# Attention kernel: the first three weight chunks of the pool projection are split in units 8, 11 and 14 instead of 5, 7 and 12

## The reference

```
s = einsum('bhqd,bhkd->bhqk', qb, kp) * scale          # 8 heads of width 64, 128 queries at a time
s = s + c[:, :, q0:q1, None] - cp[:, :, None, :]       # c: running sum of log sigmoid(forget logits)
s = where(mask, s, -1e30)
p = softmax(s, axis=-1)
outs.append(einsum('bhqk,bhkd->bhqd', p, vp))
...
y_pool = pool_mixer(u_pool, pool_w, pool_scale) @ w_pool_out     # (1024, 512) @ (512, 1024)
x = x + (g_pool * y_pool + g_fox * y_fox) @ w_out
```

## Time and profile before

| | |
|---|---|
| median of 3 runs | 1445.1 us (1444.64 to 1445.21) |
| profiled execution, its own time | 1444.98 us |
| its span, first to last instruction | 1443.1 us |
| PE busy | 98% of the span |
| DVE, ACT, POOL busy | 67%, 43%, 39% |
| mean granted TensorE clock | 0.997 of full speed (0.997 x 2.4 GHz) |
| units 0 to 31 | about 336 to 505 us of the span |

### The profile page before, as it was taken

How to read it: one execution, slowest core, us unless ns; L and a number is a source line. 1 busy time by engine, 2 the same in 40 slices (tenths; PEclk the granted TensorE clock), 3 DMA queues, 4 the chain that set the end, 5 groups by cost and what they waited for, 6 DMA issues and landing times.

```text
span 1443.1 us, 19379 instructions
## 1 busy us (share of the span) xinstructions
PE 1419.4 (98%) x7065; PEld 1171.6 (81%) x7065; DVE 971.6 (67%) x1393; ACT 618.4 (43%) x1169; POOL 557.9 (39%) x572
## 2 busy tenths in 40 slices
PE   8999999999999999999999999999999999999998
PEld 5878888887688888888888788888888888888886
DVE  7745495646877754327666887777677676775767
ACT  6545343526876642116543533332233322444445
POOL 5743233334555301005011755444444443354402
PEclk9999999999999999999999999999999999999999
DMA  8265263555333145114113213333233334883333
GB/s 213 58 120 124 54 141 86 74 103 194 111 112 114 47 161 204 59 45 146 30 44 117 74 59 110 110 109 109 83 108 109 110 110 180 310 290 96 94 103 146
DMA packets 105911, 168.45 MB, mean 117 GB/s; under 512 B 7469, under 2 KB 63297, under 8 KB 104410
## 3 DMA queue, kind: packets, MB, share of 16 engines
q1 hardware_dynamic: 99032, 147.13, 34.7%
q0 software_dynamic: 3200, 11.57, 2.2%
q10 hardware_dynamic: 3586, 8.52, 1.6%
HBM read 123.32 MB, written 42.30 MB: 115 GB/s over the span
## 4 chain that ended last, share of the span: by engine, by line
PE 89%; POOL 3%; ACT 3%; DVE 3%; issue 1%; DMA 1%; SPq 0%; DVEq 0%; ACTq 0%; POOLq 0%
PE ps L2198 27%; PE ps L2200 27%; PE ps L2199 27%; PE ps L2401 2%; PE ps L2410 1%; PE ps L2439 1%; ACT prob L1265 1%; PE ps L2440 1%; DMA raw_f<-in_w_in 1%; PE ps L2205 1%; PE ps L2269 1%; DVE prob L1801 1%; POOL w_lo L831 0%; PE ps L2574 0%; POOL tok_f L877 0%
## 5 line engine op out<-in xcount | busy, mean ns | idle before, releaser
L2198 PE MATMUL ps<-t_lo,s_hi 128*128 128x512 f32 x308 | 119.9, 389 | 0.1
L2199 PE MATMUL ps<-t_hi,s_hi 128*128 128x512 f32 x308 | 119.8, 389 | 0.0
L2200 PE MATMUL ps<-t_hi,s_lo 128*128 128x512 f32 x308 | 119.8, 389 | 0.0
L2198 PE MATMUL ps<-h_lo_T,w_hi 128*128 128x512 f32 x256 | 100.5, 393 | 1.3 <-ACT u_t L1176 1.0
L1524 DVE TENSOR_TENSOR s_lo<-w_raw,s_hi 128x512 fp32r<-128x512 f32 x77 | 59.1, 768 | 60.3 <-ACT s_hi L1439 60.1
L2200 PE MATMUL ps<-h_hi_T,w_lo 128*128 128x512 f32 x256 | 99.7, 389 | 0.0
L2199 PE MATMUL ps<-h_hi_T,w_hi 128*128 128x512 f32 x256 | 99.6, 389 | 0.0
L1439 ACT ACTIVATE s_hi<-w_raw 128x512 fp32r<-128x512 f32 x77 | 48.7, 632 | 117.7 <-PE ps L2200 99.1
L1455 ACT ACTIVATE p_sb<-ps 128x512 f32<-128x512 f32 x22 | 13.1, 598 | 189.3 <-PE ps L2200 189.3
L2198 PE MATMUL ps<-hf_lo_T,w_hi 128*128 128x512 f32 x212 | 82.5, 389 | 0.0
L2199 PE MATMUL ps<-hf_hi_T,w_hi 128*128 128x512 f32 x212 | 82.5, 389 | 0.0
(11 more groups left out here) (381 smaller groups left out, 4307.0 us busy)
## 6 DMA issues: line engine op xcount, KB each, us to landing
w_raw<-hs_dram SPq DMA_DIRECT2D x77, 256.0 KB, 2.8
raw_p<-in_w_ffn_in SPq DMA_DIRECT2D x22, 512.0 KB, 4.6
w_raw<-in_w_ffn_in SPq DMA_DIRECT2D x22, 512.0 KB, 4.3
hs_dram<-h_sum SPq DMA_DIRECT2D x11, 1024.0 KB, 8.9
hs_dram<-hq SPq DMA_DIRECT2D x11, 768.0 KB, 7.0
wq_B<-in_w_ffn_out SPq DMA_DIRECT2D x8, 1024.0 KB, 7.2
raw_f<-in_w_in SPq DMA_DIRECT2D x14, 512.0 KB, 7.2
gate_dram<-c_st SPq DMA_DIRECT2D x28, 256.0 KB, 2.2
```

The lines of the kernel that those rows point to most:

```text
L2198: nc.tensor.matmul(dst, w_h, x_l, start=start, stop=False, skip_group_check=onto)
L2199: nc.tensor.matmul(dst, w_h, x_h, start=False, stop=False, skip_group_check=onto)
L2200: return nc.tensor.matmul(dst, w_l, x_h, start=False, stop=stop, skip_group_check=onto)
```

## The change

It edits two tables and nothing else. Chunks 0, 1 and 2 of the pool projection's weights get their high part on ACT at the end of units 8, 11 and 14, where it was 5, 7 and 12. Their low part on POOL follows at the end of the same unit; it was 5, 8 and 12. SP's raw loads of chunks 2, 3 and 4 go by the same table and move to the same units. Chunks 3 to 6 keep their units 18, 23 (low part 24), 28 and 32.

```diff
-SPLIT_AT = {5: 0, 7: 1, 12: 2, 18: 3, 23: 4, 28: 5, 32: 6}
-LOW_AFTER = {5: 0, 8: 1, 12: 2, 18: 3, 24: 4, 28: 5}
+SPLIT_AT = {8: 0, 11: 1, 14: 2, 18: 3, 23: 4, 28: 5, 32: 6}
+LOW_AFTER = {8: 0, 11: 1, 14: 2, 18: 3, 24: 4, 28: 5}
```

## The result

| | before | after |
|---|---|---|
| median of 6 runs each | 1445.16 us (1444.64 to 1445.58) | 1451.82 us (1448.03 to 1452.95) |
| ratio, 95% interval | | 1.0041 [1.0029, 1.0053] |
| profiled execution | 1444.98 us | 1450.61 us |
| its span | 1443.1 us | 1448.8 us |
| PE, DVE busy | 1419.4 and 971.6 us | 1422.6 and 977.3 us |

The change makes the kernel 6.7 us slower. The forecast was 1446.4 us with 1448.2 as the end of its range. In a later group of runs the changed kernel had 1449.7 us (1447.99 to 1451.58, 7 runs) against 1445.7, so 4.0 us more, ratio 1.003 [1.0019, 1.004]. It is slower each time; and its executions lie 4.9 and 3.6 us apart in the two groups, those of before 0.9 and 4.0 (2.0 without its one slowest).

A forecast was written before the change was run, and what follows sets the result against it. PE, busy 98% of the span, was taken as the bound, so only its waits count. Terms -1.41 + 0.6 + 0.85 + 0.7 + 0.6 = +1.3 us gave 1446.4 us on the median; range 1443.5 to 1448.2 us.

The forecast's parts named there:

- The credit of unit 8: Units 5 to 8: removing chunk 0 and chunk 1's high part ends PE waits; 1.41 us gained, bounds 1.72 and 0.7.
- the copies' wait at 365.81: PE's 0.35 us wait for ACT's copies for unit 6, claimed to go without the high part at 360.97.
- Chunks 0 and 1: New places in units 8 and 11: low parts on POOL hold DVE, costing PE 0.6 and 0.85 us.
- PE's waits near 390 and 398: Sign in the profile after: these PE waits should be 0.6 and 0.9 us longer than before.
- Chunk 2's hold on k: Unit 14: the low part on POOL holds DVE's k pair, delaying unit 16's scores; cost 0.7 us, bounds -0.16 and 1.2.
- What stands behind chunk 2 on POOL: Unit 16: negc row load leaves near 415.0, so bias, za and PE's fill are late; cost 0.6 us, bounds 0 and 2.5.
- Slower, by the load behind chunk 2: Rival, unit 15: negc load waits for DVE's scalings and shares with chunk 4's load; fill waits 3.1 us, 1448.9 us; chance 0.11.
- The credit stays: Rival: new places at units 9, 12 and 15 cost PE nothing, -1.4 to -1.7 us remain, 1443.6 us; chance 0.27.
- nothing reaches PE: Rival: what the moved work delays is covered in old and new places alike, time stays at 1445.1 us; chance 0.08.
- the chance of over 0.2%: Whole kernel: chance 0.11 of being slower by more than 0.2% (2.9 us), against 0.86 for within 0.2%.

The follow-up runs named there:

- chunk 4 late, again: Kernel after the change, with SP's raw load of chunk 4 issued in unit 16 instead of 14, second group of runs: 1450.31 us, ratio 1.0032.
- behind: Kernel before, with POOL issuing unit 16's negc row load only once both DVE scalings of unit 15 are done: 1451.37 us, ratio 1.0035.
- chunk 2 alone: Kernel before, with only chunk 2 moved to unit 14, chunks 0 and 1 left in their old places: 1451.72 us, ratio 1.0043.
- the version with units 8, 12 and 15: Kernel after, with chunk 1 moved to unit 12 and chunk 2 to unit 15, chunk 0 still in 8: 1444.35 and 1444.59 us, ratios 0.9994 and 0.9995.

## Why the prediction was wrong

**The credit of unit 8: right.** -1.41 predicted, -1.28 in the profile. My 363.75 for the end of unit 6's k pair fits (363.52 + 1.40 - 1.18 = 363.74): the waits for k and for the scaled probabilities are gone there, and ACT is late next with 0.54 us where I had 0.31. Of the copies' wait at 365.81, which I had go, 0.47 us stand at 366.81; without it PE would have come sooner to the values at 373.26, where it waits for ACT anyway.

**Chunks 0 and 1: right in kind, too dear.** DVE was held where the prediction put it: the scaling of unit 9 took 1.21 us instead of 0.51 and the q instruction of unit 12 took 1.45 instead of 0.68. What reached PE is 0.24 us where I had 0.6 and 0.66 where I had 0.85. The slack that I counted half took more. I had PE's waits near 390 and 398 grow by 0.6 and 0.9 us; the first stayed at 1.42, the second grew by 0.66.

**Chunk 2's hold on k: right.** 0.69 us against 0.7; the pair took 2.86 us instead of 1.40. The Trainium skill, SBUF — State Buffer, section "Who interferes with whom", has it that a DVE instruction with two inputs in SBUF contends with a GpSimd instruction that reads SBUF, over a port pair that is locked and not shared out, and that one with at most one input there, outside the two-port modes, does not. The q and the k rows agree, and so does the bias, which reads the scores in PSUM and kept its length in the earlier trace rows. The scaling, held as well, reads one tile; that it is held rests on its row alone (1.21 us at 381.93 against 0.51).

**What stands behind chunk 2 on POOL: this step failed, in two parts.** The load went out at 416.19 - 1.18 = 415.01, just as predicted (415.0). But I let it land after the 4.28 us of before, and put the sharing of the DMA engines into the bounds only. It took 5.55 us, 1.27 more. Another 0.43 of the difference is that PE came to the fill earlier than I had it (0.31 us late where I had 0.74), since the terms of chunks 0 and 1 were smaller, and 0.27 is the way from bias to `za` and fill. 0.6 + 1.27 + 0.43 + 0.27 = 2.57, as in the profile. It lay just outside the bound of 2.5 that I had named. I named chunk 4's load as what could share, and missed the second one: q's load, released by the k pair that the same low part holds, so that both are in the air with the row by construction. By the landings q's load weighs at least as much (5.5 to 6.0 us with q alone, 5.12 with chunk 4 alone).

The second part stands nowhere in the prediction: **a wait of about 2 us or more on PE can cost the clock.** In the profile that is 1.54 us, and 1.3 to 2.5 us up to unit 18 in the seven profiles that had it. I had priced the rival's wait of 3.1 us at 3.1 us. With the terms of the profile the sum is -1.28 + 0.24 + 0.66 + 0.69 + 2.57 = +2.88 without the clock, which is 1448.0 us and still inside the range, and +4.42 with it, 1449.5, which is outside. The median of the first group, 6.7 us above, needs more than this one profile shows, and no profile of such an execution was taken. A longer landing and a clock that stays low for 6.8 us would give it: "chunk 4 late, again", "behind" and "chunk 2 alone" had such a clock and took 5.8, 5.6 and 6.9 us more than before between unit 5 and unit 18.

**The rivals.** "Slower, by the load behind chunk 2" had the place, the engine and nearly the wait (2.33 to 3.81 us against 3.1), and its chance of 0.11 was far too low. Its first reason, that the issue waits for the scalings, is refuted for the landing: 5.59 and 5.57 us beside scalings on DVE and on ACT. The rule of the Trainium skill that I gave for it (SBUF — State Buffer, section "SBUF: two separate sides") shows here as no more than 0.6 us of issuing, 1.70 against 1.10 us, and not in the landing. Its second reason, chunk 4's load beside it, is part of the answer. "The credit stays" and "nothing reaches PE" fell at 391, 399 and 416 us. What I got wrong in the chances is that the steps up to unit 15 could only add up to small sums, while the one behind chunk 2 had its far bound 4 times its value and nothing of the trace against it; there the value should have lain nearer to 2 than to 0.6, and the chance of over 0.2% near a half.

**Left open.** Landings come from one profile per kernel and differ by up to 1.5 us within a group, so the shares of q and chunk 4 are known in order only. That the clock falls in one execution and not in the next of the same kernel is seen, not explained. The 1.0 us of the version with units 8, 12 and 15 stands in both its profiles, against one of before, and its time doesn't show it beyond the noise. What moves the start of unit 5 by up to 3.7 us was not looked into.

## What to carry to other kernels

When work is moved ahead of a transfer's issue, look at which other transfers the same work releases: they will now leave together, and the landing of before isn't the price. If an instruction that another engine needs stands in order behind one that waits for a transfer, though it doesn't need it, put it ahead; here that alone left 1.4 us of a loss of 4.0 to 6.7. A single wait of about 2 us or more on a TensorE that is otherwise always busy can cost more than its length; read the granted clock in short stretches and not over the span. Scatter alone isn't the sign of it: the version with units 8, 12 and 15 scattered by 4 us too, and neither of its profiles has a fall there. Cut the span at places that all kernels have, and compare piece by piece.

## What the runs showed of the hardware

- The granted clock fell to 1.2 GHz in or just behind one gap of 1.93 to 3.81 us in a PE busy 98% of the time, in 7 of 10 profiles with such a gap, and stayed there for 3.4 us in four of them and 6.8 us in three. In the one profile with ten unread products in the gap it stayed at 2.4 GHz.
- A 512 KB load issued by POOL took 3.9 to 4.7 us from issue to read by itself or with one of 256 KB sent 1.4 us ahead, 5.12 in the one profile with one of 512 KB sent 1.5 us ahead, 5.5 to 6.0 with one of 256 KB sent 0.2 to 0.5 us ahead of it, 5.6 to 7.0 with both.
- DVE scalings beside two POOL-issued loads stretch the two issues from 1.10 to 1.70 us (to 1.47 in another kernel) and leave the landing alone.
- A subtraction on POOL over 128x1024 (2.4 us) stretches a two-instruction DVE pair from 1.40 to 2.86 us, a scaling from 0.51 to 1.21, a q instruction from 0.68 to 1.45, and leaves the bias at its usual length.
